# Two attention loops reordered and rebalanced, and the rounding of the first projections' weights moved to ScalarE

## The reference

```python
qx, kx, vx, ux = split_proj(hx @ w_in)            # hx: modulated RMS norm of x
kvc = hc @ w_in[:, ATT_DIM:3 * ATT_DIM]           # keys, values of 256 context tokens
attn_x = neighbourhood_attention(rope(qx), qx, rope(kx), vx, kc, vc, rpb)
conv_x = conformer_conv(ux, ...)                  # 31 taps over 512 channels
x = x + g1 * (concat([attn_x, conv_x]) @ w_out)
...
s = jnp.einsum('bqhd,bkhd->bhqk', q_blk, k) * scale   # second block, 8 heads
p = jax.nn.softmax(s, axis=-1)
o = jnp.einsum('bhqk,bkhd->bqhd', p, v)
```

## Time and profile before

| | before |
|---|---|
| median of 3 runs | 2766.85 us (2762.66 to 2767.86) |
| the profiled execution, its own time | 2763.07 us |
| its span, first to last instruction | 2761.0 us |
| TensorE busy | 2541.4 us (92%) |
| VectorE busy | 1375.9 us (50%) |
| ScalarE busy | 715.0 us (26%) |
| GpSimd busy | 870.6 us (32%) |
| projections, neighbourhood attention, MLA | about 50 to 335, 335 to 563, 1630 to 1859 us of the span |

### The profile page before, as it was taken

One profiled execution on the slowest core, in us unless ns is written; L12 is line 12 of the kernel. 1 busy time (PEld: TensorE's weight loads), 2 busy tenths in 40 slices (PEclk: granted clock), 3 DMA queues, 4 the chain that ended last, 5 costly groups with the idle time before them and its releaser, 6 DMA issues.

```text
span 2761.0 us, 33891 instructions
## 1 busy us (share of the span) xinstructions
PE 2541.4 (92%) x13640; PEld 2068.1 (75%) x13640; DVE 1375.9 (50%) x1463; ACT 715.0 (26%) x1044; POOL 870.6 (32%) x380
## 2 busy tenths in 40 slices
PE   6999676788999999999979989999999999999999
PEld 3788565566787887878867668878888878778777
DVE  3799967744544544444465768872012221353231
ACT  4201244431321111111144446651000020241010
POOL 1444300013343434434423200014344333523333
PEclk8999889999999999999989999999999999999999
DMA  6111344321111111111121100001111111112112
GB/s 246 39 42 58 98 139 145 109 81 46 39 46 40 53 54 47 46 47 46 53 85 46 39 8 1 2 16 46 47 61 53 47 38 54 62 39 108 45 39 91
DMA packets 54840, 165.63 MB, mean 60 GB/s; under 512 B 5348, under 2 KB 23912, under 8 KB 53288
## 3 DMA queue, kind: packets, MB, share of 16 engines
q1 hardware_dynamic: 49008, 140.68, 15.9%
q10 hardware_dynamic: 5688, 22.81, 2.1%
HBM read 152.98 MB, written 10.49 MB: 59 GB/s over the span
## 4 chain that ended last, share of the span: by engine, by line
PE 74%; DVE 18%; issue 3%; ACT 2%; DMA 2%; POOL 0%; SPq 0%; DVEq 0%; ACTq 0%; POOLq 0%
PE region L270 21%; PE region L272 21%; PE region L271 21%; DVE conv L1023 6%; PE aux L1532 2%; DVE na_prob L950 2%; PE pv L884 2%; PE pv L347 1%; DVE prob L1613 1%; DVE tmp L423 1%; PE region L851 1%; PE region L847 1%; PE region L506 1%; DMA x_sb<-x_t 1%; DVE h_lo L417 1%
## 5 line engine op out<-in xcount | busy, mean ns | idle before, releaser
L1925 POOL TENSOR_TENSOR w_hi<-w_raw,der 128x1024 fp32r<-128x1024 f32 x186 | 365.4, 1964 | 1853.5 <-PE region L272 1807.8
L270 PE MATMUL region<-h_hi,w_hi 128*128 128x512 f32 x1760 | 694.3, 394 | 41.5 <-DVE h_lo L417 20.1
L271 PE MATMUL region<-h_lo,w_hi 128*128 128x512 f32 x1760 | 689.8, 392 | 0.0
L272 PE MATMUL region<-h_hi,w_lo 128*128 128x512 f32 x1760 | 689.8, 392 | 0.0
L1928 POOL TENSOR_TENSOR w_lo<-w_raw,w_hi 128x1024 fp32r<-128x1024 f32 x186 | 504.6, 2713 | 14.6
L270 PEld LDWEIGHTS region<-h_hi,w_hi 128*128 128x128 f32 x1760 | 333.5, 189 | 112.3 <-issue 38.2
L271 PEld LDWEIGHTS region<-h_lo,w_hi 128*128 128x128 f32 x1760 | 334.0, 190 | 77.2 <-issue 8.6
L272 PEld LDWEIGHTS region<-h_hi,w_lo 128*128 128x128 f32 x1760 | 333.4, 189 | 70.3
L1023 DVE SCALAR_TENSOR_TENSOR conv<-glu,par,conv 128x1024 f32<-128x1024 f32 x120 | 198.9, 1658 | 3.1
L270 PE MATMUL region<-ff_hi,w_hi 128*128 128x512 f32 x512 | 199.2, 389 | 0.0
L271 PE MATMUL region<-ff_lo,w_hi 128*128 128x512 f32 x512 | 199.2, 389 | 0.0
(11 more groups left out here) (328 smaller groups left out, 3882.2 us busy)
## 6 DMA issues: line engine op xcount, KB each, us to landing
w_raw<-units SPq DMA_DIRECT2D x186, 512.0 KB, 3.5
w_raw<-w_ada_late SPq DMA_DIRECT2D x32, 512.0 KB, 3.6
bias<-na_bias SPq DMA_DIRECT2D x24, 384.0 KB, 3.5
ada_buf<-w_ada SPq DMA_DIRECT2D x4, 2048.0 KB, 13.4
x_sb<-x_t ACTq DMA_DIRECT2D x2, 2048.0 KB, 13.6
v_pair<-v_spill SPq DMA_DIRECT2D x64, 64.0 KB, 2.2
x<-x_t ACTq DMA_DIRECT2D x1, 4096.0 KB, 13.8
x_spill<-x ACTq DMA_DIRECT2D x1, 4096.0 KB, 11.4
```

What stands on the lines that cost most here:

```text
L270: pe.matmul(dst, wh, xh, start=first, stop=False)
L271: pe.matmul(dst, wh, xl, start=False, stop=False)
L272: return pe.matmul(dst, wl, xh, start=False, stop=last)
L1925: pool.tensor_tensor(w_hi[:, s], w_raw[:, s], one_col.broadcast_to([P, 1024]), ALU.mult)\
```

## The change

1. In the projections (units 2 to 21) ScalarE rounds the high part (`hi_after`) when the unit two before is done. GpSimd is left with the low part there. Two taps fewer in each `k`/`v`/`q` step as listed, 12 in all, so 44 taps now run beside the attention.
2. Neighbourhood attention: VectorE's negation is dropped (the sum is stored negated, with a minimum, and the exponential has scale -1); the copy of the late row and the normalisation of head 1 go to ScalarE; the orders of VectorE and ScalarE change, `lo` and `norm` now stand ahead of `most`, and the exponentials ahead of the moves. `v_pair_load` is split into four groups of four DMAs, one for a pair.
3. MLA: a second buffer `prob_odd`; values(i-2) instead of values(i-1), in another place; all four moves on ScalarE; another order on all three engines.

```diff
+    def hi_after(e, u):
+        e.wait_ge(unit_done, u + 1)
+        e.wait_ge(raw_loaded[u % 2], 16 * (u // 2 + 2))
+        copy(e, w_hi[:, u % 2], w_raw[:, u % 2]).then_inc(sem("hi_split"), 1)
+
     def u_act(e, pos, js):
...
-            e.wait_ge(unit_done, UNIT0["u"] + 2 * j + 1)
+            hi_after(e, UNIT0["u"] + 2 * j)
             e.activation(glu[:, j, PAD:PAD + T], region[:, use % 2], ACT.Sigmoid).then_inc(free[use % 2], 1)
+            hi_after(e, UNIT0["u"] + 2 * j + 1)
...
-            e.wait_ge(unit_done, UNIT0["k"] + j + 1)
+            hi_after(e, UNIT0["k"] + j)
             copy(e, k_ctx[:, j], region[:, use % 2, 0:CTX]).then_inc(free[use % 2], 1)
...
-            some_taps(7)
+            some_taps(6)
...
-            some_taps(2)
...
         for i in range(NA_N + 4):
             if i >= 4:
                 hi(i - 4)
+            if 1 <= i < NA_N + 1:
+                norm(i - 1)
             for s in range(2):
+                if i < NA_N:
+                    exps(i, s)
+                if s == 0 and i < NA_N:
+                    late_act(e, i)
                 if 2 <= i < NA_N + 2:
                     move(i - 2, s)
-                if i < NA_N:
-                    exps(i, s)
...
-            v_pair_load(sp, 1)
...
+                if i < 4:
+                    v_pair_load(sp, 1, i)
+                if TT + 3 <= i < TT + 7 or 2 * TT + 3 <= i < 2 * TT + 7:
...
-        for i in range(MLA_N + 1):
+        for i in range(MLA_N + 2):
             for s in range(2):
-                if i:
-                    turn(i - 1, s)
                 if i < MLA_N:
                     scores(i, s)
-            if i:
-                values(i - 1)
+                if s == 0 and i >= 2:
+                    values(i - 2)
+                if 1 <= i < MLA_N + 1:
+                    turn(i - 1, s)
...
             split(0, 0)
             split(0, 1)
-            split_range(2, ATTN_SPLIT)
+            with pool.Fori(1, ATTN_SPLIT // 2) as i:
+                for s in range(2):
+                    reach(pool, "hi_split", i * 2 + (s + 1))
+                    pool.tensor_tensor(w_lo[:, s], w_raw[:, s], w_hi[:, s].bitcast(F32), ALU.subtract).then_inc(unit_split, 1)
```

More of the change, by code:

```diff
@@ L1580, in mla_act @@
         for i in range(MLA_N + 1):
-            if i:
-                move(i - 1, 0, 0)
-                move(i - 1, 0, 1)
-                move(i - 1, 1, 0)
             if i < MLA_N:
                 exps(i, 0)
+            if i:
+                for n in range(4):
+                    move(i - 1, n // 2, n % 2)
+            if i < MLA_N:
+                exps(i, 1)
                 h = i // 4 + 1
@@ L1626, in store @@
                 t = 2 * (i % 4) + s
[L1627 removed]
+                last = e.tensor_copy(o_heads[rows, h // 2, t * P:(t + 1) * P], pv[64 * s:64 * s + 64, i % 2, 0:P])
                 if s:
@@ L1895, in _ @@
             reach(sp, "v_spill1", 32)
-            v_pair_load(sp, 0)
+            for cs in range(4):
+                v_pair_load(sp, 0, cs)
             late_load(0)
```

120 lines of the change are left out of this document (55 added, 65 removed).

## The result

| | before | after |
|---|---|---|
| median of 4 runs | 2766.74 us | 2697.07 us (2694.4 to 2697.55) |
| ratio | | 0.9749, 95% interval [0.9732, 0.9766] |
| profiled execution: span, own time | 2761.0, 2763.07 us | 2695.0, 2696.8 us |

A forecast was written before the change was run, and what follows sets the result against it. Only TensorE's waits at the projections' end, in the attention and in MLA could give time back. Gains 8 + 8 + 41 + 13.5 = 70.5 from 2763.07 gave 2692.6, so a median of 2696 us, range 2678 to 2722.

The forecast's parts named there:

- Term 1: Start of the projections: unit 2 waits for ScalarE's rounding ahead of the sigmoid, +1.0 us (0 to +2.5).
- the upper end: Start of the projections: if GpSimd's low part doesn't fit beside the sigmoid and comes last, up to +2.5 us.
- before units 3 to 21: Projections: gaps of TensorE ahead of these units were named as a sign that the forecast is wrong.
- the starvation rival: Projections: ScalarE's late rounding stops TensorE in each of 20 units, 4 us lost in each, 2776 us; chance 0.03.
- Term 2: End of the projections: VectorE is on time, first attention sum at 326.4, -8 us (-10 to -5), term 1 included.
- Term 3: First pairs of the attention: TensorE's wait for late weights goes, -8 us (-11 to -4).
- the wait of 8.53: Start of the attention: TensorE waits 8.53 us for late weights, whose load stands behind 16 DMAs on SyncE's queue.
- Term 4: Remaining 28 attention pairs: values no longer wait for scores, 5.35 for 6.82 a pair, -41 us (-54 to -23).
- The new cycle: Attention pair: ScalarE's high part, VectorE's low part to first sum, ScalarE's exponentials, late row and moves; 5.1 with one tap.
- ScalarE paces: Attention: ScalarE's multiply enters the cycle, 0.25 more a pair, 2703 us, or 2713 with more hand-overs; chance 0.13.
- Term 5: MLA: the wait for normalised probabilities goes, 31 pairs x 0.5 less 2 at the ends, -13.5 us (-18 to 0).

The follow-up runs named there:

- run 4: Changed kernel with the projections' high parts rounded on GpSimd again, 80 taps kept there; ratio 0.9738 to the kernel before.
- run 7: Changed kernel, ScalarE still rounding, with 92 taps in the projections again; ratio 0.9738 to the kernel before.
- run 8: Changed kernel with the 16 DMAs of the second pair's values in one block ahead of the pairs; ratio 0.9759 to the kernel before.
- run 12: Changed kernel with late row on VectorE, 101 taps in the projections, third late weights loaded ahead of the biases; ratio 0.9673 to the kernel before.
- run 6: Changed kernel with the copy of the late row on VectorE behind the first maximum; ratio 0.9739 to the kernel before.
- run 1: Kernel before with only the changed attention and its SyncE loads; ratio 0.9814 to the kernel before.
- run 3: Kernel before with only the changed projections: ScalarE's rounding and 80 taps; ratio 0.9984 to the kernel before.
- run 9: Changed kernel with the late row on VectorE and 101 taps in the projections; ratio 0.9685 to the kernel before.

## Why the prediction was right

All terms against the two profiled executions, which are 66.0 apart in span:

| term | predicted | measured |
|---|---|---|
| start, ahead of anything edited | 0 | -1.3 |
| 1 and 2, first sum of the attention, from the start | -8 | -6.9 |
| 3, first four pairs | -8 | -4.2 |
| 4, other pairs, and the attention's tail | -41 | -42.65 - 0.5 |
| 5, MLA | -13.5 | -13.1 |
| attention's end to MLA's start | 0 | -3.15 |
| behind MLA | 0 | +5.8 |

**Term 1.** Predicted +1.0 with 2.5 as its far end. Counted from the start, TensorE takes up unit 2 1.0 later and is 2.1 later at its last matmul of the projections. At unit 2 it was the low part that came last, as the remark on the upper end had it (changed kernel, waits, 80 to 100 us; columns: total, times, longest):

```profile
PEld region L272 <- POOL w_lo L1954: 4.4, 1, 4.4
```

The second 1.1 is a wait that the prediction put at nothing ("so I count nothing"). From 102 to 235 us TensorE runs 132.05 of 133 us, all of them before, and the missing 0.95 is one gap, ahead of unit 3 (changed kernel, TensorE):

```profile
103.40 0.47 PE L272 MATMUL region<-h_hi,w_hi 128*128 128x512 f32 x1 [0.95 <-DVE glu L656]
```

VectorE's product for `glu` (L656), which frees a half of `region`, starts 3.2 later than before, counted from the start. Ahead of it stands the preparation of the context, now behind ScalarE's second rounding (89.58, 1.05) and beside GpSimd's low parts: two of VectorE's products of 128x256 take 2.12, where they took 0.76. All 53 us from 235 to 288 are busy. So the gap "before units 3 to 21" occurs once, for 1 us, and not in each unit: the starvation rival gets no more than that.

**Term 2.** The time, 326.28 for 326.4, is right in part by luck: the profiled execution started 1.3 earlier, and term 1 was 1.1 larger. The copies of the last unit end at 319.17 for 319.4, and from there the 7.1 to the first sum is as predicted (7.0). Counted from the start the gain is 6.9 for 8. The account behind it, 27 for the high parts and 15.4 for the taps, was larger than needed: it said that VectorE would then wait for TensorE, not that either would do alone (runs 4 and 7). The taps average 1513 ns, near the 1.5 named. 77 x (1.51 - 1.28) = 18 us of turns with the low parts remain.

**Term 3** was mis-sized: -4.2 for -8. The step that failed is "so the wait of 8.53 goes; I give 0.5 back". The block of 16 was not all that stood ahead of the late weights; 3.69 stayed, for three biases and full DMA engines (runs 8 and 12). The low clock of the first pairs was there, 0.75 over the four, and with it the chain of matmuls and sums that run 12 shows to be left when the load is early.

**Term 4** was right in mechanism and size: 5.14 and 5.62 for 5.1 and 5.7, 143.15 / 27 = 5.30 for 5.35. (The table has the 27 intervals from pair 4 to the last pair; the prediction counted 28 pairs, at 6.82 where the mean of these is 6.88.) The new cycle sets the pairs with one tap, VectorE's own work those with two. The multiply took 830 ns for 0.8 and was on no path: in the pair shown it ends 0.50 before the exponential starts. *ScalarE paces* asked for 0.25 a pair more; that was not seen. But run 6 shows that ScalarE's late row was in the cycle with at least 0.45, and the first estimate counted 0.28 for it.

**Term 5**: right in sum, with two errors that cancel. From the first maximum of the first pair to that of the last, 31 pairs, the time falls from 215.0 to 201.9: 6.94 and 6.51 a pair (6.43 predicted), 13.1 in sum for 15.5. From there to the last heads both kernels take 13.7, where I had put 2 on. The "0.5 in a pair", counted from an issue, was too much: the earlier trace rows has (221 - 208.33) / 31 = 0.41 for a pair, and 6.94 - 0.41 = 6.53. No run has one part of MLA's change alone (the second buffer, the place of the values, the fourth move), so which of them removes the wait is argued and not shown.

**Outside the stages** I had counted nothing, and the two profiled executions differ by -3.15 and +5.8. The change moves no instruction there. Behind MLA the records show the granted clock low for 10.2 us from 2489, for 3.4 at 2562 before. The other runs speak for chance, and for the kernel before as the one that stands out: it takes 1067.7 from the attention's end to MLA and 901.9 behind MLA, while the 13 others, with the same code there, take 1060.9 to 1067.4 and 904.0 to 909.0, also runs 1 and 3, which keep the old MLA (909.0 and 907.0).

The sum was 70.5 where 66.0 came: term 3 short by 3.8, terms 1 and 2 by 1.1, term 5 by 0.4, and 1.35 lost outside and at the start, against 2.15 more in term 4. The median still lay within 1.1 of the forecast, because it was only 0.3 above the profiled execution, and I had carried over the 3.8 of the kernel before. That close a hit is luck; the medians are 69.7 apart.

## What to carry to other kernels

When two edits relieve the same engine, look for the slack that either would leave: here the rounding or the 12 taps would have done. The taps, moved into the next stage, cost some 6 there, and the rounding on top of them put the first sum 2.4 later. Before two traces are compared, take out what differs ahead of the first edit. Find the cycle that sets a repeating pair, and count every hand-over in it, also an engine's wait for its own result; work taken out of it pays in every pair even if it goes to a fuller engine, until that engine or TensorE is the bound. Where a load is late, look at what is ahead of it both on its queue and in the transfers, one load at a time: the largest block may not be the last obstacle.

## What the hardware showed that was not expected

- A copy of 128x128 on ScalarE cost at least 0.45 of the pair, not its 0.25: the next instruction waited another 0.17 for its result.
- VectorE loses the more time to GpSimd the more GpSimd does beside it. With both of GpSimd's splits a tap averaged 1769 ns (run 4), with the low part alone 1513, and with neither 1279. The Trainium skill ("SBUF — State Buffer", SBUF: two separate sides) calls the port that both use an exclusive lock, held for a whole instruction. The trace agrees: the taps in the earlier trace rows end 1.09 and 1.11 after GpSimd's instruction that they met, less than one tap's time.
- TensorE's busy time is not a fixed cost of a pair. I counted 4.86 for it, from the old kernel at a granted clock of 0.98; in run 9 pairs of 4.62 and 4.69 ran, with TensorE busy almost without a pause. In the changed kernel it is 110.40 x 5.30 / 124 = 4.72. I take it, and haven't shown it, that a part of each wait is counted as busy, since the ends of matmuls are modelled; the busy time of a pair with waits would then be more than the pair needs.
